# Key and value products by quarters, weight sums in place, and the memory's transposes inside the output projection, in an fp32 encoder layer

## The reference, cut to what matters

```python
h = h + concat([y_r, y_a]) @ w_out            # y_r: RWKV-7 mixing, y_a: windowed attention; w_out 2048 x 2048
hn = rms_norm(h, norm_xatt)
mem_n = rms_norm(mem, mem_norm)               # memory: 256 rows x 2048
q = (hn @ wq); k = (mem_n @ wk); v = (mem_n @ wv)      # each 2048 x 512, 4 heads of 128
h = h + softmax(q k^T / sqrt(128)) v @ wo
h = h + experts(rms_norm(h, norm_moe))        # 32 experts (4 groups of 8), each three 4 MB matrices
out = rms_norm(h, final_norm)
```

## Time and profile before

| | |
|---|---|
| three runs, us | 1790.73, 1792.40, 1794.39 |
| profiled execution: its own time, span | 1793.52, 1791.7 us |
| busy: PE, DVE, ACT, POOL | 1692.2, 618.9, 338.2, 124.7 us |
| mean granted TensorE clock | 0.992 of full speed |
| DMA share of 16 engines, 900 to 1791 us | 0.98, 416 GB/s |
| chain that ended last | PE 70%, DMA 21%, DVE 4% |

### The profile page before, as it was taken

The page is one execution under the profiler, slowest core; times in us unless marked ns, Lnnn a source line. Parts: engine busy times, 40 slices in busy tenths (PEclk is TensorE's granted clock), DMA queues, the critical chain, the costliest instruction groups (busy, mean ns, idle before and its releaser), DMA issues.

```text
span 1791.7 us, 36478 instructions
## 1 busy us (share of the span) xinstructions
PE 1692.2 (94%) x15655; PEld 1123.0 (63%) x15655; DVE 618.9 (35%) x1330; ACT 338.2 (19%) x966; POOL 124.7 (7%) x206
## 2 busy tenths in 40 slices
PE   8999999989998999999999999999999999999996
PEld 7887888877777888576554554445444545454543
DVE  2001333488887462023123222232223222322233
ACT  2112222157666101122000000000000000000002
POOL 1000000013235000001000000000000000000000
PEclk9999999999999999999999999999999999999999
DMA  9932434300000944436999999999999999999995
GB/s 304 220 113 94 121 118 175 110 3 4 4 4 4 338 169 158 186 157 242 415 393 425 432 427 434 426 434 429 430 429 432 430 429 430 430 432 424 409 421 208
DMA packets 100783, 503.59 MB, mean 281 GB/s; under 512 B 38204, under 2 KB 42704, under 8 KB 81472
## 3 DMA queue, kind: packets, MB, share of 16 engines
q1 hardware_dynamic: 95960, 489.22, 68.2%
q0 software_dynamic: 4464, 12.03, 2.3%
q10 hardware_dynamic: 248, 0.65, 0.1%
HBM read 511.29 MB, written 4.23 MB: 288 GB/s over the span
## 4 chain that ended last, share of the span: by engine, by line
PE 70%; DMA 21%; DVE 4%; issue 2%; SPq 1%; ACT 1%; POOL 1%; DVEq 0%; ACTq 0%; POOLq 0%
PE ps L1734 15%; DMA rest<-in_wd 9%; DMA ring<-in_wu 9%; PE ps L2288 8%; PE ps L2280 8%; PE ps L2431 8%; PE ps L2064 5%; PE ps L2296 4%; DMA rest<-in_wu 2%; PE ps L2116 2%; PE ps L2167 2%; PE ps L2184 2%; PE ps L2125 2%; DMA ring<-in_wg 1%; PE ps L1951 1%
## 5 line engine op out<-in xcount | busy, mean ns | idle before, releaser
L1734 PE MATMUL ps<-wide,ring 128*128 128x256 f32 x1248 | 275.3, 379 | 1.2 <-PE ps L1734 0.9
L1734 PEld LDWEIGHTS ps<-wide,ring 128*128 128x128 f32 x1248 | 239.0, 195 | 39.7 <-issue 10.1
L2288 PE MATMUL ps<-ring,wide 128*64 128x256 f32 x1472 | 170.8, 391 | 28.9 <-DMA ring<-in_wu 28.7
L1594 DVE TENSOR_TENSOR tokA<-tokA,ps 128x512 f32<-128x512 f32 x256 | 158.5, 682 | 102.1 <-PE ps L2296 102.1
L2280 PE MATMUL ps<-ring,wide 128*64 128x256 f32 x1600 | 178.8, 381 | 2.9 <-DVE wide L1582 1.9
L1607 DVE SCALAR_TENSOR_TENSOR gg<-ps,tmp,gg 128x256 f32<-128x256 f32 x32 | 15.5, 484 | 472.4 <-PE ps L2288 472.4
L2431 PE MATMUL ps<-ring,gg 128*64 128x512 f32 x736 | 168.1, 598 | 0.8 <-DMA ring<-in_wd 0.8
L2288 PEld LDWEIGHTS ps<-ring,wide 128*64 128x64 f32 x1472 | 107.7, 141 | 91.3 <-DMA ring<-in_wu 36.9
L2280 PEld LDWEIGHTS ps<-ring,wide 128*64 128x64 f32 x1600 | 113.6, 137 | 60.2 <-DVE wide L1582 3.3
L2296 PE MATMUL ps<-wide,gg 64*128 64x512 f32 x512 | 135.3, 627 | 0.6 <-ACT wide L926 0.6
L2431 PEld LDWEIGHTS ps<-ring,gg 128*64 128x64 f32 x736 | 48.7, 136 | 114.5 <-issue 106.9
(11 more groups left out here) (381 smaller groups left out, 2203.7 us busy)
## 6 DMA issues: line engine op xcount, KB each, us to landing
ring<-in_wu SPq DMA_DIRECT2D x20, 4096.0 KB, 29.5
ring<-in_wg SPq DMA_DIRECT2D x19, 4096.0 KB, 28.4
ring<-in_wd SPq DMA_DIRECT2D x19, 4096.0 KB, 30.8
rest<-in_wd SPq DMA_DIRECT2D x8, 4096.0 KB
ring<-in_w_in SPq DMA_DIRECT2D x7, 4096.0 KB, 16.4
rest<-in_wg SPq DMA_DIRECT2D x6, 4096.0 KB
rest<-in_wu SPq DMA_DIRECT2D x6, 4096.0 KB
ring<-in_w_out SPq DMA_DIRECT2D x4, 4096.0 KB, 19.5
```

The lines of the kernel that those rows point to most:

```text
L1594: V.tensor_tensor(fin_part(t, h, n), fin_part(t, h, n), ps[:, banks[q][h], :], ALU.add).then_inc(S["added"], 1)
L1734: ins = mm(ps[0:rows_, m % 2, 0:T], lhs, hnT[:, k, :], start=k == 0, stop=k == KD - 1)
L2288: ins = mm(ps[CAP * h:CAP * h + CAP, 1, 0:T], xT[:, k, CAP * i:CAP * i + CAP], w[:, T * h:T * h + T], start=k == 0, stop=k == KD - 1)
```

## The change

1. Keys and values are formed by the same seven products of quarters, with the memory as A and `wk`, `wv` as B, as blocks 4 and 5. The memory's own quarters are read from `memT`, its sums go to `rest` and `oT` (four sums of 1024 elements on VectorE after block 3). Both come out with rows as rows; the keys' rows (`krow` in `tmp`) are then turned by eight transposes, in two groups inside block 5. Values are summed straight into `vx`.
2. The weight sums T1, T2, T3, T4 go to the places of B11, B22, B12, B21 themselves, so each is formed inside its own block, when the product that reads the raw quarter is done. The order of products on TensorE is 1, 2, 3, 5, 7, 6, 4 in all blocks (block 0: 2, 1, 3, 5, 7, 6, 4, with the variance matmul after two steps of product 2). None is formed during the last pair.
3. The memory is turned in eight rounds of four transposes, all into bank 0, each after a product in blocks 2 and 3; ScalarE alone takes each round out.
4. The second norm (`normed(2)`) comes inside block 4 on VectorE.

The diff, cut to its core:

```diff
@@ ScalarE
-            turned(1)
+            for r in range(KD // 2):
+                act.wait_ge(S["hn_tr"], KD // 2 + r + 1)
+                for c in (2 * r, 2 * r + 1):
+                    src = ps[:, 0, T * (c % 2):T * (c % 2) + T]
+                    ins = A(memT[:, c, :], src, ACT.Copy, scale=prm[:, P_MEM + c:P_MEM + c + 1])
+                ins.then_inc(S["hn_ev_a"], 1)
...
-            for f in range(4):
-                act.wait_ge(S["xk_mm"], f + 1)
-                A(kxT[:, f, :], ps[:, f, 0:T], ACT.Copy).then_inc(S["xk_ev"], 1)
-            for b in range(TB):
-                act.wait_ge(S["xk_mm"], 5 + b)
-                A(vx[:, b, :], ps[:, 4 + b, :], ACT.Copy).then_inc(S["xk_ev"], 1)
+            for n in range(2):
+                act.wait_ge(S["xk_mm"], n + 1)
+                A(kxT[:, 2 * n:2 * n + 2, :].rearrange("p f t -> p (f t)"), ps[:, 0, :], ACT.Copy).then_inc(S["xk_ev"], 1)
@@ VectorE
-                V.tensor_tensor(W_T1, W_B12(n), W_B11(n), ALU.subtract).then_inc(S["w_t"], 1)
...
+            def w_t1(n, k=slice(0, CT)):
+                ins = V.tensor_tensor(W_B11(n)[:, k], W_B12(n)[:, k], W_B11(n)[:, k], ALU.subtract)
+                if k.stop == CT:
+                    ins.then_inc(S["w_t"], 1)
...
+            def w_t2(n):
+                dve.wait_ge(*later("w_t", 4 * n + 2))
+                V.tensor_tensor(W_B22(n), W_B22(n), W_B11(n), ALU.subtract).then_inc(S["w_t"], 1)
...
-                if last:
-                    w_t1(0)
-                    w_t2(0)
...
-                if last:
-                    w_t3(0)
-                    w_t4(0)
...
+                dve.wait_ge(landed[where[L_OUT + n]], arrived[L_OUT + n])
                 if n == 0:
+                    made(n, 1)
                     w_add(n, 0, 0, product(2))
+                    dve.wait_ge(*later("w_p1", 1))
+                    w_t1(n, slice(0, CT - 1))
+                    made(n, 2)
                     w_op(W_U, product(1), None)
                     w_add(n, 0, 0, W_U)
+                    w_t1(n, slice(CT - 1, CT))
+                else:
+                    made(n, 1)
+                    w_op(W_U, product(1), None)
+                    w_add(n, 0, 0, W_U)
+                    w_t1(n)
+                    made(n, 2)
+                    w_add(n, 0, 0, product(2))
+                w_t3(n)
+                made(n, 3)
+                w_add(n, 0, 1, product(3))
+                w_t2(n)
+                w_t4(n)
...
+            dve.wait_ge(S["hn_ev_a"], 12)
+            V.tensor_tensor(M_S1, M_S3, M_A22, ALU.add).then_inc(S["w_s7"], 1)
...
+            memory_block(4, krow)
+            memory_block(5, vx)
@@ TensorE
+            def combined_products(n, s1, s2, s3, a22):
+                pe.wait_ge(*later("w_t", 4 * n + 1))
+                product(n, 5, s1, W_B11(n))
+                if n in (2, 3):
+                    memory_turn(4 * n - 5)
+                pe.wait_ge(*later("w_t", 4 * n + 2))
+                product(n, 7, s3, W_B12(n))
+                pe.wait_ge(*later("w_t", 4 * n + 3))
+                product(n, 6, s2, W_B22(n))
+                pe.wait_ge(*later("w_t", 4 * n + 4))
+                product(n, 4, a22, W_B21(n))
+                pe.wait_ge(S["op_mm"], 7 * n + 7)
+                pe.sem_inc(used[where[L_OUT + n]], 1)
+
+            def memory_turn(r):
+                if r == 0:
+                    pe.wait_ge(S["hn_done"], 2)
+                else:
+                    pe.wait_ge(S["hn_ev_a"], 4 + r)
+                for c in (2 * r, 2 * r + 1):
+                    for b in range(TB):
+                        o = T * (c % 2) + P * b
+                        ins = tr(ps[:, 0, o:o + P], memtok[:, b, P * c:P * c + P], ident)
+                ins.then_inc(S["hn_tr"], 1)
+
             landing(L_OUT)
-            pe.wait_ge(*later("w_t", 4))
-            pe.wait_ge(*later("w_s", 2 * (CT - 1)))
-            product(0, 1, W_A11, W_B11(0), first)
+            product(0, 2, W_A12, W_B21(0), range(0, 2))
             pe.wait_ge(S["rw_dsq"], CT)
             mm(ps[:, 7, T:2 * T], ones2, DSQ, start=True, stop=True).then_inc(S["rw_var"], 1)
...
+            landing(L_K)
+            product(4, 1, M_A11, W_B11(4))
+            product(4, 2, M_A12, W_B21(4))
+            pe.wait_ge(*later("w_s7", 8))
+            product(4, 3, M_S4, W_B22(4))
+            combined_products(4, M_S1, M_S2, M_S3, M_A22)
             landing(L_V)
+            product(5, 1, M_A11, W_B11(5))
+            product(5, 2, M_A12, W_B21(5))
+            pe.wait_ge(S["op_add"], W_BASE[5])
+            keys_turned(0)
+            product(5, 3, M_S4, W_B22(5))
+            pe.wait_ge(S["xk_ev"], 1)
+            keys_turned(1)
+            combined_products(5, M_S1, M_S2, M_S3, M_A22)
```

More of the change, by code:

```diff
@@ L1366, in w_add, with made @@
                 w_op(tokA[:, b, o:o + T], tokA[:, b, o:o + T], x)
+            def made(n, count):
+                dve.wait_ge(S["op_mm"], 7 * n + count)
             w_ops = [0]
@@ L1389, in _ @@
[L1389 to L1400, removed]
@@ L2056, in _, with product @@
             mm(ps[:, 7, 0:T], ones2, Yp, start=True, stop=True).then_inc(S["rw_mu"], 1)
-            def product(n, i, lhs, rhs, ks=range(CT)):
-                if n >= 1 and ks[0] == 0:
-                    pe.wait_ge(S["op_add"], W_EACH * (n - 1) + (W_READ if n >= 2 else W_READ0)[i])
+            def product(n, i, lhs, rhs, ks=range(CT), ends=True):
+                if n >= 1:
+                    pe.wait_ge(S["op_add"], W_BASE[n - 1] + (W_READ0, W_READ, W_READ, W_READ, M_READ)[n - 1][i])
                 for k in ks:
@@ L2100, in _ @@
-                product(n, 4, W_A22, W_T4)
-                pe.wait_ge(S["op_mm"], 7 * n + 7)
-                pe.sem_inc(used[where[L_OUT + n]], 1)
-            pe.wait_ge(S["op_add"], W_ADDS)
-            pe.wait_ge(S["hn_done"], 2)
-            turn(1)
-            pe.wait_ge(S["hn_ev_a"], 8)
-            pe.wait_ge(S["hn_ev_v"], 8)
-            def features(n, x, count):
-                landing(n)
-                s = where[n]
-                for f in range(4):
-                    for k in range(KD):
-                        ins = mm(ps[:, f, 0:T], slot_k(s)[:, k, P * f:P * f + P], x[:, k, :], start=k == 0, stop=k == KD - 1)
-                    ins.then_inc(S["xk_mm"], 1)
-                pe.wait_ge(S["xk_mm"], count)
-                pe.sem_inc(used[s], 1)
@@ L2121, in _ @@
-            features(L_K, memT, 4)
-            landing(L_V)
-            for b in range(TB):
-                for k in range(KD):
-                    ins = mm(ps[:, 4 + b, :], memT[:, k, P * b:P * b + P], slot_k(where[L_V])[:, k, :], start=k == 0, stop=k == KD - 1)
-                ins.then_inc(S["xk_mm"], 1)
-            pe.wait_ge(S["xk_mm"], 6)
-            pe.sem_inc(used[where[L_V]], 1)
-            pe.wait_ge(S["xk_ev"], 6)
+                if n >= 2:
+                    memory_turn(4 * n - 7)
```

141 lines of the change are left out of this document (71 added, 70 removed).

## The result

| | before | after |
|---|---|---|
| median of the runs, us | 1792.8 (4 runs) | 1801.86 (4 runs, 1800.59 to 1805.26) |
| profiled execution: its own time, span | 1793.52, 1791.7 | 1800.59, 1798.4 |
| mean granted TensorE clock | 0.992 | 0.979 |
| packets on the instruction queue | 94 | 139 |
| first expert load goes out | 751.01 | 741.36 |

The ratio is 1.0054, 95% interval 1.0037 to 1.0072: slower, where I had put a chance of 0.87 on faster. The last two lines of the table say where to look. The first expert load went out 9.65 us earlier; the way from it to the end is 16.3 us longer.

The account below looks back on a forecast made before the run. A stream of expert-weight transfers sets the end, its start hanging on TensorE. 7.1 + 3.9 - 1.2 = 9.8 us less than the profiled 1793.5 gives 1783.7, or 1782.6 as median; stated 1783, range 1779.5 to 1787.5.

Parts of the forecast that it names:

- Keys and values: After the last projection product: seven products each for keys and values bring 61.60 us to 54.5, 7.1 less.
- rival C: New blocks: VectorE's sums come late, keys' product 3 waits 2.9 us, product 5 another 2; time 1789, chance 0.06.
- rival E: Eight memory and two keys' transpose rounds: TensorE's clock falls, 1.7 us each, 17 for all; time 1800, chance 0.04.
- The last pair: Last pair of heads: without four VectorE sums, POOL's steps and TensorE's wait shorten, 3.9 us less.
- Rival A: Last pair of heads stays long, POOL or clock late for another reason; gain only 0.7 us, time 1786, chance 0.12.
- The gap of 0.86 ahead of the first mark: TensorE idle just before the last pair's measured stretch; if it went too, that gain would reach 4.8 us.
- The first block: Output projection's first block: TensorE waits for a weight sum, block ends at 26.5 instead of 25.3, costing 1.2 us.
- The wait before product 5: First output projection block: product 5 waits for T1's last eighth from 11.7 to 12.7, about 1 us.
- The sum at the first expert load: First expert load goes out at about 741 instead of 751, from terms summing to 9.8 us less.
- time saved on TensorE ahead of 751 moves the whole stream and with it the end: Expert loads: releases hang on TensorE's place in the program, so time saved before 751 us moves the end too.
- B: Expert weight loads: the stream of transfers swallows the whole gain; time 1792.4, chance 0.06.
- the same distance from there to the end: Sign: from the first expert load, at about 741 instead of 751, to the end takes as long as before.

Follow-up runs that it names:

- TINY = 57: Kernel after with 57 small matmuls (228 instructions) added at TensorE's very start: 1785.99 us, single run.
- TINY = 27: Kernel before with 27 small matmuls (108 instructions) added at TensorE's very start: 1815.83 us, ratio 1.0133.
- TINY = 50: 50 small matmuls (200 instructions) added at TensorE's start: kernel before 1792.32 us, ratio 0.9998; kernel after 1782.4 us, ratio 0.9936.
- TINY = 3: Kernel after with 3 small matmuls (12 instructions) added at TensorE's very start: 1809.67 us, single run.
- TINY = 5: Kernel after with 5 small matmuls (20 instructions) added at TensorE's very start: ratio 0.9950, runs of 1782.27, 1784.57 and 1785.48 us.
- TINY = 37: Kernel after with 37 small matmuls (148 instructions) added at TensorE's very start: 1782.95 us, ratio 0.9944.
- TINY 0 and 64: Kernel after without added matmuls, 1801.86 us, and with 64 small matmuls (256 instructions) at TensorE's very start, 1801.72 us.

## Why the prediction was wrong, by its own steps

**Keys and values: right.** Between the last projection product (691.23 less the gap of 0.30) and the next turn lie 50.87 us; with 2 x 1.75 for the memory's rounds 54.37, forecast 54.5. The gain is 7.2, forecast 7.1. VectorE kept ahead: the longest stretch that worried me, the four sums of 1024, ran 1.22 each, and TensorE never waits for VectorE before product 3 or 5 of the keys (rival C). TensorE's clock never moved there, with the ten small turns inside (windows of after):

```profile
640.00:690.00 50.00, 49.70 (x247) 43.48 (x246) 28.16 (x32) 6.71 (x16) 3.93 (x5) 1.00 0.51 173
690.00:742.00 52.00, 50.83 (x239) 43.88 (x238) 32.05 (x31) 5.59 (x8) 0.00 (x0) 1.00 0.44 162
```

So rival E, the one on the slower side, is refuted, though the time it gave, 1800, is close to what came. The two numbers agree by chance; the mechanism of E had nothing to do with it.

**The last pair: right.** From POOL's group at line 543 (547.65; before 547.91, rows 9) to the mean's matmul it takes 38.76 instead of 42.62: 3.9 less, forecast 3.9. Rival A falls. The gap of 0.86 ahead of the first mark stayed (0.79). The experiment that puts the sums back gives 4.2. That the forecast is met to a tenth is partly luck, for the stretch varies by 1.7 us between executions without the sums. The granted clock is 1.00 through the last pair, as I had said (POOL's last steps and windows of after):

```profile
576.89 1.14 POOL L543 TENSOR_TENSOR ring<-ring,cst_sb 128x128 f32<-128x128 f32 x3 [0.35 <-ACT ring L785]
```
```profile
575.00:580.00 5.00, 4.56 (x120) 3.28 (x120) 0.00 (x0) 4.06 (x15) 3.67 (x9) 1.00 0.02 7
580.00:585.00 5.00, 4.62 (x170) 3.83 (x164) 1.99 (x9) 1.93 (x9) 1.44 (x2) 1.00 0.22 33
```

**The first block: right in kind, 0.35 off.** 27.16 from the mean to block 1 instead of 25.61: 1.55 more, forecast 1.2. The wait before product 5 is 0.88, forecast 1.0; taking it out gives back 1.15. Product 5 began 12.75 after the mean, forecast 12.7. The miss lies behind it: the last four products took 14.08 where I counted four times 3.45, 13.8. A whole block takes 24.43, 0.28 more than seven times 3.45, and I had left that out.

**The sum at the first expert load: right.** 7.2 + 3.9 - 1.55 = 9.55; the load came 9.65 earlier at 741.36, forecast "about 741".

**The step that failed: "time saved on TensorE ahead of 751 moves the whole stream and with it the end".** I took the stretch from the first load to the end as a constant of 1040.7 us, gave a lengthening of it no price and no rival (B only has the stream swallow the gain), and named "the same distance from there to the end" as a sign; it was 1057.0. The runs show what was left out: the change also moved the experts' loop within TensorE's program, from about 147 to about 241 of a block, by the stalls' records 94 instructions (107 by my count from the program; I can't say where the 13 went). Five back edges then cost 48.9 us of missing code and, by the busy time of L2318 (195.4 us in after, 178.8 with the loop moved), 16.6 us of slow matmuls: 65.5 us, of which 17.8 reach the end (1057.0 against 1039.2). The rest fell mostly on time that TensorE had spent on transfers: with the loop moved it waits 30.0 us for them (22.7, 4.4 and 2.9 in the three largest rows), and the busy time of L2326 is 173.1 us where it is 164.1 in after; some 9 us I have not placed. With the loop moved the prediction holds within two microseconds: forecast 1783, medians 1782.95, 1782.4 and 1784.57.

One slip in the working: the range's upper end of 1787.5 does not follow from rival A at its lower bound, which gives 1792.4 - 7.1 + 1.2 = 1786.5. The result lies above either.

What would have shown it beforehand: the page of before lists the instruction queue, 94 packets, and the diff adds a known number of matmuls to TensorE ahead of a loop that fills most of eight blocks. A rival "the loop moves to a place where it is fetched again" had its row there and would have been the slower side of the chances. By the table about 40 to 70 of 256 places stall: 213 and above do, 185 and below don't, and between them nothing was measured.

## What to carry to other kernels

Count an engine's instructions as well as its work: where a loop of many matmuls closes the kernel, an edit far ahead of it can decide whether its code is still there at the back edge. Read the instruction queue's packets and the "issue" waits of both kernels before blaming an edit, and test with padding at a free place; a change judged without this would have been thrown away here, 0.5% slower, while it is worth 0.5 to 0.6% at a good place. And compare the way to a mark and the way from it apart: nine and a half microseconds gained as forecast on the way to the mark, and sixteen lost on the way from it, where nothing had been edited, showed at once where to look.

## What the hardware showed that I had not expected

- Instruction packets of 16.4 KB; a stall of 6.0 to 7.3 us for the first one at a back edge (6.4 us in after, 7.3 with TINY = 57), beside weight transfers that kept the DMA engines at 0.98 of their time, and 60.1 us for five back edges at the worst place (the kernel before, TINY = 27), against none for the same loop 92 instructions further on (TINY = 50). In the kernel after, the 8 instructions from TINY = 3 to TINY = 5 decide it.
- Once the first block is missing, nine packets come in each pass (45 at five edges), but only the first two are waited for. The body lies in eight blocks there; by count, the ninth packet is the block behind it. A body that ends by about 86 of its eighth block never stalls, at 114 it does at two of five edges, from 142 on always.
- The packets' times show what decides; which block a packet brings I count from the table's places. In the kernels with five stalls the block behind the body, the ninth, comes 5 to 7 us ahead of the first back edge (after 1050.02, edge 1055.54; TINY = 3 1055.19, edge 1060.57; before with TINY = 27 1058.01, edge 1064.76). In the kernel before and with TINY = 37 it doesn't come, and no packet follows until the loop is left. With TINY = 5 the body lies in seven blocks: the block behind it, the eighth, comes at 1050.91 and costs nothing. With TINY = 57 no packet comes at three edges; at the fourth two come together, at 1415.15 and 1415.86, 2.4 us after TensorE has stopped. So eight blocks of 256 instructions are kept, and a ninth costs the first. That the fetch of a block starts about halfway through the one before it, I only argue, from stalls at 142, two of five at 114 and none at 86.
- The Trainium skill, "Runtime: NRT & Kernel Launch", section "Instruction fetch mechanics", gives 128 KiB for TensorE, refilled in blocks of 16 KiB with 256 instructions, and says that a taken branch whose target is outside the current two pages forces a fetch. Block size and the period of 256 agree with the runs (16.4 KB; TINY 0 and 64), and 128 KiB are eight such blocks, as many as the packets' times show to be kept. The two pages don't agree: a body of 1693 instructions, 6.6 blocks, jumps back in the kernel before without one packet or stall.
- Two executions with identical text (TINY = 50) differ by 4.2 us in span, all of it ahead of the last pair's mean: 1.3 us before the pairs of heads begin, 1.2 in the first seven pairs and 1.7 in the last.
